# Moving turned blocks between partitions without DRAM: sixteen SBUF-to-SBUF DMAs in place of one out and four back

## The reference

```python
h = h + retention_layer(h, ...)      # 8 heads, q/k 256 wide, v 512 wide, gated, w_out
h = h + pooling_layer(h, ...)        # windows 2, 4, 8, 16, a grouped matmul, gated, w_out
x = rms_norm(h, final_norm)
x = x + concat([out_mla, out_diff]) @ w_out     # latent attention and differential attention
x = x + cross_attention(x, mem) @ w_xo
x = x + (silu(hf @ w_gate) * (hf @ w_up)) @ w_down    # hidden width 5632
return rms_norm_2(x, g_final)
```

## Time and profile before

| | |
|---|---|
| Median of 3 runs | 2507.16 us |
| The profiled execution, its own time | 2508.08 us |
| Its span | 2506.3 us |
| TensorE clock granted | 0.999 of full |
| Busy: TensorE, DVE, ACT, POOL | 99%, 63%, 48%, 7% |
| DMA share in most fortieths of the span | 0.6 to 0.7 |
| Read from HBM, written to it | 507.23 MB, 34.08 MB |

### The profile page before, as it was taken

How to read it: one execution, slowest core, us unless ns; L and a number is a source line. 1 busy time by engine, 2 the same in 40 slices (tenths; PEclk the granted TensorE clock), 3 DMA queues, 4 the chain that set the end, 5 groups by cost and what they waited for, 6 DMA issues and landing times.

```text
span 2506.3 us, 29305 instructions
## 1 busy us (share of the span) xinstructions
PE 2493.3 (99%) x11088; PEld 2060.9 (82%) x11088; DVE 1577.5 (63%) x1970; ACT 1214.2 (48%) x1531; POOL 185.9 (7%) x309
## 2 busy tenths in 40 slices
PE   9999999999999999999999999999999999999998
PEld 7888788888888888888888888888888888888887
DVE  7565665665666666675767766776655555555556
ACT  6454444444445453444545556465544444444444
POOL 0010000000010100000001100010100000000000
PEclk9999999999999999999999999999999999999999
DMA  9676666666687877776777754675766666666664
GB/s 330 206 229 212 212 210 204 217 208 199 218 235 227 243 223 230 228 233 210 218 244 243 238 163 152 229 228 192 237 216 210 201 209 218 203 215 204 214 205 146
DMA packets 261740, 542.81 MB, mean 217 GB/s; under 512 B 13440, under 2 KB 19712, under 8 KB 261248
## 3 DMA queue, kind: packets, MB, share of 16 engines
q1 hardware_dynamic: 240992, 477.32, 58.9%
q0 software_dynamic: 20496, 63.98, 9.3%
q10 hardware_dynamic: 144, 0.06, 0.0%
HBM read 507.23 MB, written 34.08 MB: 216 GB/s over the span
## 4 chain that ended last, share of the span: by engine, by line
PE 98%; DVE 1%; DMA 1%; ACT 0%; issue 0%; POOL 0%; ACTq 0%; DVEq 0%
PE job L1998 31%; PE job L1999 31%; PE job L2004 31%; PE group L2022 1%; DMA rqn<-across 0%; PE att L2292 0%; PE att L2043 0%; PE att L2293 0%; PE group L2314 0%; PE att L2188 0%; PE att L2057 0%; PE att L2056 0%; PE att L2053 0%; PE att L2036 0%; DMA across<-rtmp 0%; PE att L2173 0%
## 5 line engine op out<-in xcount | busy, mean ns | idle before, releaser
L1173 DVE TENSOR_TENSOR lo<-raw,hi 128x1024 fp32r<-128x1024 f32 (+1 forms) x880 | 1054.8, 1215 | 665.8 <-ACT hi L671 650.2
L671 ACT ACTIVATE hi<-raw 128x1024 fp32r<-128x1024 f32 (+1 forms) x880 | 921.9, 1055 | 1111.3 <-PE job L2004 1101.9
L1998 PE MATMUL job<-hi,xh 128*128 128x512 f32 (+1 forms) x2272 | 888.0, 391 | 1.9 <-DVE xl L1209 1.6
L1999 PE MATMUL job<-hi,xl 128*128 128x512 f32 (+1 forms) x2272 | 881.5, 388 | 0.0
L2004 PE MATMUL job<-lo,xh 128*128 128x512 f32 (+1 forms) x2272 | 605.1, 388 | 0.0
L1998 PEld LDWEIGHTS job<-hi,xh 128*128 128x128 f32 x2272 | 426.4, 188 | 92.6 <-issue 3.0
L1999 PEld LDWEIGHTS job<-hi,xl 128*128 128x128 f32 x2272 | 426.9, 188 | 88.4 <-issue 2.1
L2004 PEld LDWEIGHTS job<-lo,xh 128*128 128x128 f32 x2272 | 425.6, 188 | 87.5
L1998 PE MATMUL job<-hi,ah 128*128 128x512 f32 x832 | 326.1, 392 | 0.0
L1999 PE MATMUL job<-hi,al 128*128 128x512 f32 x832 | 323.9, 389 | 0.0
L2004 PE MATMUL job<-lo,ah 128*128 128x512 f32 x832 | 222.5, 389 | 0.0
(11 more groups left out here) (330 smaller groups left out, 1215.1 us busy)
## 6 DMA issues: line engine op xcount, KB each, us to landing
raw<-in_ret_w_in SPq DMA_DIRECT2D x95, 1024.0 KB, 5.2
raw<-in_pool_w_in SPq DMA_DIRECT2D x64, 1024.0 KB, 6.2
raw<-in_w_gate SPq DMA_DIRECT2D x44, 1024.0 KB, 5.2
raw<-in_w_up SPq DMA_DIRECT2D x44, 1024.0 KB, 5.1
raw<-in_w_down SPq DMA_DIRECT2D x44, 1024.0 KB, 5.0
raw<-in_ret_w_out SPq DMA_DIRECT2D x32, 1024.0 KB, 5.1
raw<-in_pool_w_out SPq DMA_DIRECT2D x32, 1024.0 KB, 5.3
raw<-in_w_in SPq DMA_DIRECT2D x28, 1024.0 KB, 5.6
```

The costliest lines, as they stand in the source:

```text
L671: act.activation(hi[:, (U.at * 2 + h) % HS, :, 0:n], src, ACT.Copy).then_inc(hi_ready, 1)
L1173: dve.tensor_tensor(lo[:, (U.at * 2 + h) % LS, :, 0:n], src, hi[:, (U.at * 2 + h) % HS, :, 0:n].bitcast(F32), ALU.subtract).then_inc(lo_re ...
L1998: pe.matmul(o, oh[:, kt, ts], w, start=first and k == 0, stop=False)
L1999: pe.matmul(o, ol[:, kt, ts], w, start=False, stop=False)
```

## The change

POOL no longer writes the block to DRAM. In place of one DMA of 128 partitions out and four of 32 partitions back, it issues sixteen DMAs, each from 32 partitions of the block buffer to 32 partitions of the destination, 32 KB each, with no wait between them. `t_out` is gone. A crossing is done when `t_in` has counted 16 times 16 more, and every wait that was on `t_out` is on that full count of the crossing before. All waits on `t_in` go from 64 a crossing to 256. The diff, with the lines where only 64 becomes 256 left out after the first:

```diff
-        across = [nc.dram_tensor(f"across{n}", (TT * P, 4, 4 * BK), F32).ap() for n in range(2)]
...
             sp.wait_ge(group_filled, DO_G[3] + 1)
-            sp.wait_ge(t_out, 16 * (NQ + 1))
+            sp.wait_ge(t_in, 256 * (NQ + 1))
...
             def turn_across(n, blk, turned):
 
                 pool.wait_ge(t_blocked, n + 1)
-                if n >= 2:
-                    pool.wait_ge(t_in, 64 * (n - 1))
-                pool.dma_start(across[n % 2].rearrange("(t p) q c -> p t (q c)", p=P),
-                               blk.rearrange("p t q c -> p t (q c)")).then_inc(t_out, 16)
-                pool.wait_ge(t_out, 16 * (n + 1))
                 for q in range(4):
-                    pool.dma_start(turned[BK * q:BK * (q + 1), :, :],
-                                   across[n % 2][:, q, :].rearrange("(b i) c -> i b c", i=BK)).then_inc(t_in, 16)
+                    for b in range(4):
+                        to = turned[BK * q:BK * (q + 1), :, :].rearrange("p (t b) c -> p t b c", b=4)
+                        pool.dma_start(to[:, :, b, :], blk[BK * b:BK * (b + 1), :, q, :]).then_inc(t_in, 16)
...
-                act.wait_ge(t_in, 64 * (n + 1))
+                act.wait_ge(t_in, 256 * (n + 1))
...
             def blocks(n, blk, src):
 
                 if n:
-                    dve.wait_ge(t_out, 16 * n)
+                    dve.wait_ge(t_in, 256 * n)
...
-                    dve.wait_ge(t_out, 16 * ret_turned(i, 0))
+                    dve.wait_ge(t_in, 256 * ret_turned(i, 0))
...
-                dve.wait_ge(t_out, 16 * NQ)
+                dve.wait_ge(t_in, 256 * NQ)
...
-                dve.wait_ge(t_out, (I + (NF - TF)).value(16))
+                dve.wait_ge(t_in, (I + (NF - TF)).value(256))
```

More of the change, by code:

```diff
@@ L285, in build @@
         u_landed, m_mixed, m_high, m_low = sem("u_landed"), sem("m_mixed"), sem("m_high"), sem("m_low")
-        t_blocked, t_out, t_in, t_high, t_low = sem("t_blocked"), sem("t_out"), sem("t_in"), sem("t_high"), sem("t_low")
+        t_blocked, t_in, t_high, t_low = sem("t_blocked"), sem("t_in"), sem("t_high"), sem("t_low")
         xt_high, xt_low, rk_ready, dq_ready = sem("xt_high"), sem("xt_low"), sem("rk_ready"), sem("dq_ready")
@@ L693, in x_across @@
             def x_across(m, c, gain, col):
-                act.wait_ge(t_in, 64 * (NX[m] + c + 1))
+                act.wait_ge(t_in, 256 * (NX[m] + c + 1))
                 for k in range(4):
@@ L857, in pad_group @@
                 n = 2 * i + c
-                act.wait_ge(t_in, 64 * (NP + 4 * i + c + 1))
+                act.wait_ge(t_in, 256 * (NP + 4 * i + c + 1))
                 if n:
@@ L1100, in hidden_high @@
             def hidden_high(I, dst):
-                act.wait_ge(t_in, (I + (NF - TF)).value(64))
+                act.wait_ge(t_in, (I + (NF - TF)).value(256))
                 act.activation(dst[:, 0:4, :].rearrange("p k (b c) -> p k b c", c=BK),
@@ L2072, in ret_turn @@
                     U, J = U + 4, J + 1
-                pe.wait_ge(t_in, 64 * (ret_turned(i, 0) + 1))
+                pe.wait_ge(t_in, 256 * (ret_turned(i, 0) + 1))
                 pe.wait_ge(rk_ready, i + 1)
@@ L2199, in behind_input @@
                     pe.wait_ge(dq_ready, 1)
-                    pe.wait_ge(t_in, 64 * (ND + 2))
+                    pe.wait_ge(t_in, 256 * (ND + 2))
                     diff_scores(0)
@@ L2210, in behind_input @@
                     pe.wait_ge(dq_ready, 2)
-                    pe.wait_ge(t_in, 64 * (ND + 4))
+                    pe.wait_ge(t_in, 256 * (ND + 4))
                     diff_scores(2)
```

## The result

The changed kernel takes 2554.01 us (median of 5 runs, 2552.80 to 2555.09), beside 2507.16 us for the kernel before on the same chip: ratio 1.0188, 95% interval 1.0177 to 1.0199. It is slower by 47 us. The profiled execution has a span of 2553.3 us, 47.0 more than before, and a granted clock of 0.992.

The account below looks back on a forecast made before the run. TensorE, busy 99% of the span, was taken as the bound. Stalls of 4.6 + 7.6 + 14.3 + 14.9 = 41.4 us, the 1.6 us recovery included, on the median 2507.2 gave 2548.6, written as 2548; range 2522 to 2592.

Parts of the forecast that it names:

- What can be gained: TensorE's only wait on a turned block, before L1998 at the end of the retention tail: 1.6 us.
- the four named places: Retention tail +4.6 us, pooling tail +7.6, ahead of cross attention +14.3, ahead of the feed-forward block +14.9.
- SP's wait: SP's wait at L556 moves to the landing, at most T less 4 us later; costed at nothing.
- the consumers: Users of the turned data, served at about the same time as before; waits costed at nothing except the 1.6 us.
- the bytes: Software queue traffic falls from 63.98 MB by 32.0 MB; costed at nothing, being hidden behind the matmuls.
- The wait as the cause: DVE's single block buffer now waits for all sixteen landings, delaying the `lo` splits that TensorE needs; sum +41.4 us.
- T: Length of a crossing: fifteen issues of 0.58 us plus a landing of 4.7, 13.4 us; ends 11.7 and 16.0.
- The cover: At a tail's accumulate the next `lo` is due 7.25 us later; TensorE stalls only for what exceeds it.
- The stalls: TensorE's stalls behind late `lo` splits or `xl` in four places; nine terms move with T, about 9 us per microsecond.
- Short crossings: Rival: an issue costs by its bytes, 0.15 us, so T is 6.9 and the time 2507 us; chance 0.09.
- the queue that falls behind: Rival: an issue or landing slot takes 1.2 us, so T is 22.7 and the time 2675 us; chance 0.12.
- the larger cover: Rival: `lo` splits run more than two halves ahead and absorb DVE's stalls; 2506 to 2507 us; chance 0.04.

Follow-up runs that it names:

- the kernel with the four places as before: Changed kernel, but the 13 crossings of the four close-crossing places go through DRAM with the old waits, the other 48 new; 2513.34 us, ratio 1.0024.
- the second buffer: Changed kernel with the second of two close crossings going to another, idle block buffer, so DVE waits for the crossing before the last; 2506.03 us, ratio 0.9997.
- the wait alone: Kernel before, DRAM copies kept, with every wait on `t_out` outside POOL put on the full `t_in`; 2553.04 us, ratio 1.0185.
- eight and by twenty-four copies: Changed kernel with eight copies of 64 KB a crossing, 2530.95 us; and with eight of the sixteen copies cut in two, 2604.99 us.
- the four bare holds: Kernel before, TensorE held at four places by a chain of 36 memsets on POOL; 2541.26 us, ratio 1.0136.
- a filled hold: Kernel before with the same four memset holds, each filled with 20 extra matmuls on TensorE; 2530.50 us, ratio 1.0095.

## Why the prediction was right, and where it was off

The forecast was 2548 us, the range 2522 to 2592; it is 2554. Step by step:

- **What can be gained.** 1.6 us, and it is gone, as said.
- **The places.** Stalls only in the four named places. The 48 other crossings, SP's wait, the consumers and the bytes were costed at nothing: 0.7 us was lost outside, and the kernel with the four places as before shows no wait in the other 48 crossings, though it lost 6.5 us to a pause and a slow copy in one of its old ones.
- **The wait as the cause.** Right, and shown from both sides, by the second buffer and by the wait alone.
- **T.** 13.4 us assumed, 12.4 in the mean. Fifteen issues took 7.87 for 8.7 (0.525 us each for 0.58), the landing 4.5 in the mean for 4.7, scattered from 1.75 to 6.44. The row of an issue with four times the bytes was the right neighbour. The rival in which an issue costs by its bytes is ruled out by eight and by twenty-four copies, at 0.525 and 0.50 us an issue.
- **The cover.** The rule "the next `lo` is due 7.25 us after the accumulate" held. Retention tail: transposes at 721.68, so the first split is done at 724.06, due 715.32 + 7.25 = 722.57; 1.5, measured 1.6. Second: 740.21 + 1.15 less 728.11 + 7.25 is 6.0, measured 6.2.
- **The stalls.** Predicted 43.0 in sum, measured 31.6 (1.6 and 6.2; 1.4 and 5.6; 3.4 and 3.4; 4.1 and 5.9). A microsecond less of T was priced at 9, which gives 34. The largest error is ahead of cross attention, 14.3 predicted and 6.8 measured: the first crossing took 10.6 us and not 13.4, and its 2.8 us are missing from the second stall also. The third stall vanished. In the pooling tail the row at 1320.12 held one of POOL's pauses: it stands 4.3 us behind its accumulate, against 2.9 in the retention tail and 2.9 in this place after, so the sum took 1.4 us of pause for post.
- **The missing term.** The sum let TensorE go on at full pace after a stall. It doesn't: 15.4 us. This is the step that failed, by omission. It hides behind the over-counted stalls: 31.6 + 15.4 - 1.6 = 45.4, against 41.4 (the other 1.6 us of the 47.0 are the short waits elsewhere), and the total looks better than its parts. That 2548 came so near to 2554 is in part luck: stalls put 11.4 us too high made up for most of a term of 15.4 us that was left out. The retention tail shows it plainly (4.6 predicted, 8.2 measured); ahead of cross attention (14.3, 13.1) both errors cancel.
- **The pauses.** Two of POOL's fell on crossings that count (710.46 and 1819.04), 3.4 us each. Not foreseen, though the rows of before had one. What they cost in the 47 us was not measured.
- **The skill's rules.** Landings overlapped, as the row said: T of 9.6 to 14.3 us speaks against paying the fixed 2.0 us of the Trainium skill (DMA: Bandwidth & Descriptors, Anatomy of one DMA) sixteen times in a row, which gave 33. Of that page's lower latency without HBM something shows: over the whole span the least landing fell from 3.0 to 1.7 us and the median from 5.1 to 4.2, about half of the 2 us that I had taken from it. The new copies carry a quarter of the bytes as well, so how much of this is due to DRAM isn't told apart.
- **Rivals.** Short crossings failed by the issue's price, the queue that falls behind by T, the larger cover by the stalls.

## What to carry to other kernels

When a copy is shortened or a buffer's path changes, ask first what event frees the source buffer; here "copied out" became "landed", and that alone was worth 47 us, while half the traffic was worth nothing. A second buffer for the close pairs removes the cost. Price a stall of TensorE at its length plus the slow stretch behind it (here 2.5 to 2.6 us behind stalls of 3.4 us and more, nothing behind those of 1.4 and 1.6), but expect only a part of it back if the next stall is set by another chain.

## What was unexpected of the hardware

- POOL's issue of a small SBUF-to-SBUF copy of 32 partitions takes 0.53 us whether it carries 32 or 64 KB; the landings overlap, and the last of eight larger copies lands later after its issue than the last of sixteen (6.3 us in the mean against 4.5).
- POOL stands still now and then, with its wait met: in the kernel after for 3.4 us at intervals of 128 copies, in the kernel before for about 1.7 us at intervals of 55 to 60. 96 more satisfied waits didn't move it; with 96 foreign copies ahead one pause was added and the others kept their crossings. The cause is open.
- Satisfied waits on POOL, some 0.04 us each, ran 22 us ahead of the memset that they stood before, though a wait on TensorE stood ahead of them in the program. Whether the build or the engine does that wasn't looked into; a chain of memsets makes a delay (5.58 us for 36).
- TensorE's granted clock was 0.50 behind each of the four bare holds of 5.9 us and the six stalls of 3.4 to 6.2 us, for 4 to 7 us. Behind stalls of 1.4 and 1.6 us, and behind the 1.2 us left of a filled hold, it was 1.00 and matmuls went on every 0.23 to 0.24 us.
